# Rotary halves in the two late layers: matrix products on TensorE replaced by exchanges on SyncE's DMA queue, and four key products made two

## The reference, cut to what matters

```python
def apply_rope(x, cos, sin):
    x1, x2 = jnp.split(x, 2, axis=-1)
    rot = jnp.concatenate([-x2, x1], axis=-1)
    return x * cos + rot * sin

def apply_axial_rope(x, row_cs, col_cs):          # kind A, on each half of a head of 64
    half = x.shape[-1] // 2
    return concat([apply_rope(x[..., :half], *row_cs), apply_rope(x[..., half:], *col_cs)])

kv = einsum('bsr,rc->bsc', rms_norm(ckv, c_kvn), c_wukv).reshape(b, s, C_HEADS, C_NOPE + C_V)
kc_nope = kv[..., :C_NOPE]                        # the latent keys: 4 heads of 64 features
```

## Time and profile before

| what | value |
|---|---|
| median of three executions | 1819.11 us |
| the profiled execution's own time | 1817.71 us |
| its span in the profile | 1815.9 us |
| TensorE busy | 1764.0 us (97%) |
| VectorE, ScalarE, GpSimd busy | 797.8, 722.8, 603.9 us |
| mean granted TensorE clock | 0.989 of full speed |

### The profile page before, as it was taken

One profiled execution on the slowest core, in us unless ns is written; L12 is line 12 of the kernel. 1 busy time (PEld: TensorE's weight loads), 2 busy tenths in 40 slices (PEclk: granted clock), 3 DMA queues, 4 the chain that ended last, 5 costly groups with the idle time before them and its releaser, 6 DMA issues.

```text
span 1815.9 us, 25198 instructions
## 1 busy us (share of the span) xinstructions
PE 1764.0 (97%) x10862; PEld 1389.8 (77%) x10862; DVE 797.8 (44%) x1342; ACT 722.8 (40%) x1228; POOL 603.9 (33%) x182
## 2 busy tenths in 40 slices
PE   8999999999999999998999999989999999999997
PEld 5778899987888888877888888878675478766456
DVE  7756656623123120113680044135636654526653
ACT  5746565433233332223331122224336543345541
POOL 3434210333333334433354444433432115233112
PEclk9999999999999999998999999989999999999999
DMA  5130200315223322222232222223220012211001
GB/s 206 70 94 24 73 3 25 133 70 192 80 96 105 122 70 99 110 71 92 79 106 93 93 93 95 105 79 118 93 70 24 1 47 99 93 50 67 1 1 47
DMA packets 37503, 144.70 MB, mean 80 GB/s; under 512 B 3155, under 2 KB 15835, under 8 KB 23696
## 3 DMA queue, kind: packets, MB, share of 16 engines
q1 hardware_dynamic: 18944, 121.53, 18.7%
q10 hardware_dynamic: 18448, 21.57, 4.0%
HBM read 140.93 MB, written 5.30 MB: 81 GB/s over the span
## 4 chain that ended last, share of the span: by engine, by line
PE 91%; DVE 4%; ACT 2%; issue 1%; DMA 1%; ACTq 0%; POOL 0%; POOLq 0%; SPq 0%; DVEq 0%
PE bank L407 57%; PE bank L1145 7%; PE bank L613 5%; PE bank L418 4%; PE bank L2196 3%; PE bank L2220 3%; PE bank L2203 2%; PE bank L1653 1%; PE bank L1629 1%; PE bank L668 1%; PE bank L2228 1%; PE bank L2149 1%; ACT w_part L365 1%; PE bank L439 1%; DVE WK L978 0%
## 5 line engine op out<-in xcount | busy, mean ns | idle before, releaser
L407 PE MATMUL bank<-x_part,w_part 128*128 128x512 f32 x3216 | 747.1, 392 | 1.6 <-ACT WK L2309 0.8
L407 PEld LDWEIGHTS bank<-x_part,w_part 128*128 128x128 f32 x3216 | 601.2, 188 | 135.3 <-issue 10.3
L2660 POOL TENSOR_TENSOR w_part<-RAW,w_part 128x2048 fp32r<-128x2048 f32 (+1 forms) x90 | 404.2, 4494 | 676.6 <-ACT w_part L365 674.7
L365 ACT ACTIVATE w_part<-RAW 128x2048 fp32r<-128x2048 f32 (+1 forms) x90 | 165.8, 1842 | 176.3 <-PE bank L407 138.0
L2660 POOL TENSOR_TENSOR w_part<-WK,w_part 128x2048 fp32r<-128x2048 f32 (+1 forms) x30 | 123.7, 4123 | 248.6 <-ACT w_part L365 248.6
L407 PE MATMUL bank<-f_part,w_part 128*128 128x512 f32 x768 | 174.4, 389 | 0.0
L407 PEld LDWEIGHTS bank<-f_part,w_part 128*128 128x128 f32 x768 | 144.1, 188 | 29.9
L1145 PE MATMUL bank<-WK 64*64 64x64 f32 (+1 forms) x1456 | 102.0, 248 | 5.1 <-ACT WK L1311 3.4
L1145 PEld LDWEIGHTS bank<-WK 64*64 64x64 f32 (+1 forms) x1456 | 97.8, 162 | 7.3 <-ACT WK L1311 3.5
L978 DVE SCALAR_TENSOR_TENSOR WK<-bank,COL,WK 128x510 f32<-128x510 f32 (+1 forms) x96 | 71.7, 748 | 48.1 <-ACT WK L920 45.5
L2677 POOL TENSOR_TENSOR WK<-BASE,WK 128x1024 f32<-128x1024 f32 x16 | 30.4, 1898 | 160.0 <-DVE WK L2503 111.8
(11 more groups left out here) (286 smaller groups left out, 2230.8 us busy)
## 6 DMA issues: line engine op xcount, KB each, us to landing
RAW<-wts SPq DMA_DIRECT2D x83, 1024.0 KB, 4.8
WK<-wts SPq DMA_DIRECT2D x23, 1024.0 KB, 4.8
WK<-scratch ACTq DMA_DIRECT2D x16, 256.0 KB, 2.7
WK<-decay_rows ACTq DMA_DIRECT2D x14, 256.0 KB, 6.9
RAW<-wts SPq DMA_DIRECT2D x7, 512.0 KB, 3.5
WK<-wts SPq DMA_DIRECT2D x7, 512.0 KB, 3.4
scratch<-bias_rows ACTq DMA_DIRECT2D x4, 768.0 KB, 9.8
WK<-xT SPq DMA_DIRECT2D x4, 512.0 KB, 6.0
```

The lines of the kernel that those rows point to most:

```text
L365: act.eng.activation(high_part(i), raw_part(i), ACT.Copy).then_inc(*act.did(("hi", i)))
L407: mm = pe.eng.matmul(b[:, :], W[w][:, k, c:c + P], src[x][k], start=start and k == 0 and n == 0, stop=stop and k == kn - 1 and n == 2)
L2660: eng.tensor_tensor(low_part(i), raw_part(i), high_part(i).bitcast(F32), ALU.subtract).then_inc(w_split, 1)
```

## The change

1. Within each head of 64 the features of the kinds A and B are reordered on the host, so that the partner of a feature always lies 32 partitions away (`HALVES`, for A; B has that distance already). The cosine and sine tables are reordered alike, and the sign of the half turn moves into the sine tables.
2. The eight rotation products of a layer, and the matrices `ra` and `rb`, are gone. In their place SyncE issues eight DMAs per layer, SBUF to SBUF, four for `QKF` tiles 0 to 3 and four for tiles 4 to 7. Each moves 32 partitions by 4 x 512 float32 (256 KB) to the neighbouring 32 partitions of `XCH`, which is the place of the gates' tile `GTM`, still unused then. They stand in the queue just ahead of the load of the second piece of G0.
3. VectorE's `rope` reads `XCH` in place of PSUM. Rotations 0 to 3 stand ahead of the first `grow`, 4 to 6 behind the first three, 7 behind the fifth.
4. ScalarE's squares of C no longer wait for `ropes`. TensorE waits for it ahead of the attention.
5. The four latent key products of 64 rows become two of 128 rows; ScalarE still makes four copies, two from each.

```diff
-            pe.wait_ge(*at(("tabs", l)))
             pe.wait_ge(*at(("small", l)))
-            for i in range(8):
-                pe.wait_ge(*at((L, "qn", i)))
-                b = job((L, "rot", i))
-                E.matmul(b[:, :], tab("ra") if i < 4 else tab("rb"), QKF[:, i, :], start=True, stop=True).then_inc(*pe.did(("pe", (L, "rot", i))))
             for i in range(3):
                 fm((L, "C", i), f"L{l}C", i * P, HTS)
...
-            for h in range(4):
-                b = job((L, "uk", h))
-                E.matmul(b[0:64, :], UKV[:, h * 64:(h + 1) * 64], CL[:, 2, :], start=True, stop=True).then_inc(*pe.did(("pe", (L, "uk", h))))
+            for j in range(2):
+                b = job((L, "uk", j))
+                E.matmul(b[:, :], UKV[:, j * P:(j + 1) * P], CL[:, 2, :], start=True, stop=True).then_inc(*pe.did(("pe", (L, "uk", j))))
             gates(0)
             gates(1)
 
             pe.wait_ge(*at((L, "kready")))
             pe.wait_ge(*at((L, "qready")))
+            pe.wait_ge(*at((L, "ropes")))
...
             for i, m in enumerate((P, 64, P)):
-                act.wait_ge(*at((L, "ropes")))
                 act.wait_ge(*at((L, "ccp", i)))
...
-            def rope(dst, rot, c, s, tmp, m, rel, lab):
-
-                dve.wait_ge(*at(("pe", rot)))
-                V.tensor_tensor(tmp[0:m], ps(rot)[0:m, :], s[0:m], ALU.mult).then_inc(*dve.did(free=rot))
-                V.tensor_tensor(dst[0:m], dst[0:m], c[0:m], ALU.mult).then_inc(*dve.did())
+            def rope(i):
+
+                k = i // 4
+                x, y = QKF[:, i, :], XCH[:, i, :]
+                dve.wait_ge(*at(("turned", l, k)))
+                V.tensor_tensor(y, y, tab(("asn", "bs")[k]), ALU.mult).then_inc(*dve.did())
+                V.tensor_tensor(x, x, tab(("ac", "bc")[k]), ALU.mult).then_inc(*dve.did())
                 dve.wait_ge(*dve.last())
-                V.tensor_tensor(dst[0:m], dst[0:m], tmp[0:m], ALU.add).then_inc(*dve.did(*lab))
+                V.tensor_tensor(x, x, y, ALU.add).then_inc(*dve.did(*([(L, "ropes")] if i == KO - 1 else [])))
...
-            for j in range(4):
+            for i in range(4):
+                rope(i)
+            for j in range(3):
                 grow(j)
+                rope(4 + j)
+            grow(3)
             for h in range(4):
                 dve.wait_ge(*at((L, "cqc", h)))
             rope_c(CQ, SQL, 4, [(L, "qready")])
-            for j in range(4, KO):
+            grow(4)
+            rope(7)
+            for j in range(5, KO):
                 grow(j)
...
+            exchange_at = {(f"L{l}G0", 256): l for l in range(LAYERS)}
             for i, (_, _, k, n) in enumerate(subs):
+                if subs[i][:2] in exchange_at:
+                    l = exchange_at[subs[i][:2]]
+                    sp.wait_ge(*at(("pe", (f"lay{l}", "sum", 0))))
+                    for h in range(2):
+                        for j in range(4 * h, 4 * h + 4):
+                            sp.wait_ge(*at((f"lay{l}", "qn", j)))
+                        for b in range(4):
+                            frm = b ^ 1
+                            eng.dma_start(XCH[32 * b:32 * b + 32, 4 * h:4 * h + 4, :], QKF[32 * frm:32 * frm + 32, 4 * h:4 * h + 4, :])\
+                                .then_inc(turned_in[l][h], 16)
                 if i >= RAW_SLOTS:
                     sp.wait_ge(*at(("subfree", i - RAW_SLOTS)))
```

More of the change, by code:

```diff
@@ L50 @@
 TURNED = [*range(16, 32), *range(16)]
+HALVES = [*range(16), *range(32, 48), *range(16, 32), *range(48, 64)]
 MIXED = [12, 13, 6, 9, 0, 3, 14, 15, 7, 10, 1, 4, 8, 11, 2, 5]
@@ L117, in rope_tables @@
     return np.cos(ang).T.astype(np.float32), np.sin(ang).T.astype(np.float32)
[L120 to L129, removed]
 def shape_constants():
@@ L150, in shape_constants @@
     for n in range(2):
-        ax = np.concatenate([axr[n], axc[n]], 0)
+        ax = np.concatenate([axr[n], axc[n]], 0)[HALVES]
         tabs.append(np.concatenate([ax, ax], 0))
@@ L154, in shape_constants @@
         tabs.append(np.concatenate([one_d[n], one_d[n]], 0))
+    for x in (tabs[1], tabs[3]):
+        x[0:32] *= -1.0
+        x[64:96] *= -1.0
     for n in range(2):
@@ L168 @@
 TAB = dict(ac=(0, 512), asn=(512, 512), bc=(1024, 512), bs=(1536, 512), cc=(2048, 512), cs=(2560, 512),
-           ra=(3072, 128), rb=(3200, 128), win=(3328, 384))
-NTAB = 3712
+           win=(3072, 384))
+NTAB = 3456
 NGDN = 7 * P + 64
@@ L320, in build @@
         bias_in = [sem(f"bias_in{i}") for i in range(2)]
+        turned_in = [[sem(f"{k}_halves_exchanged{l}") for k in "ab"] for l in range(LAYERS)]
         out_done = sem("out_done")
@@ L323, in build @@
         rows_in = [sem(f"decay_rows_in{u}") for u in range(8)]
-        for s in [rows_out, bias_rows_out, *rows_in, *w_in_slot, w_split, const_in, gdnc_in, wgate_in, sel_in, *x_in, x_again, tabs_in, *small_in, *bias_out, *bias_in, out_done]:
+        for s in [rows_out, bias_rows_out, *rows_in, *w_in_slot, w_split, const_in, gdnc_in, wgate_in, sel_in, *x_in, x_again, tabs_in, *small_in, *bias_out, *bias_in, *turned_in[0], *turned_in[1], out_done]:
             byname[s.name] = s
@@ L341, in build @@
             table[("small", l)] = (small_in[l], 16)
+            for k in range(2):
+                table[("turned", l, k)] = (turned_in[l][k], 64)
         def weights(chunk, c):
@@ L2069, in build @@
         GTM = wk(25600, KO, S)
+        XCH = GTM
         MIX = parts("mix_part", 15360, KO, S)
@@ L2307, in lay_act @@
             for h in range(4):
-                act.wait_ge(*at(("pe", (L, "uk", h))))
-                A.activation(CK[0:64, h, :], ps((L, "uk", h))[0:64, :], ACT.Copy).then_inc(*act.did(*([(L, "kready")] if h == 3 else []), free=(L, "uk", h)))
+                j, o = divmod(h, 2)
+                act.wait_ge(*at(("pe", (L, "uk", j))))
+                A.activation(CK[0:64, h, :], ps((L, "uk", j))[64 * o:64 * o + 64, :], ACT.Copy)\
+                    .then_inc(*act.did(*([(L, "kready")] if h == 3 else []), free=(L, "uk", j) if o else None))
             for g in range(2):
@@ L2417, in lay_dve @@
             dve.wait_ge(*at(("tabs", l)))
-            def rope(dst, rot, c, s, tmp, m, rel, lab):
-                dve.wait_ge(*at(("pe", rot)))
-                V.tensor_tensor(tmp[0:m], ps(rot)[0:m, :], s[0:m], ALU.mult).then_inc(*dve.did(free=rot))
-                V.tensor_tensor(dst[0:m], dst[0:m], c[0:m], ALU.mult).then_inc(*dve.did())
+            def rope(i):
[4 more added lines that the diff above has]
+                V.tensor_tensor(x, x, tab(("ac", "bc")[k]), ALU.mult).then_inc(*dve.did())
                 dve.wait_ge(*dve.last())
-                V.tensor_tensor(dst[0:m], dst[0:m], tmp[0:m], ALU.add).then_inc(*dve.did(*lab))
+                V.tensor_tensor(x, x, y, ALU.add).then_inc(*dve.did(*([(L, "ropes")] if i == KO - 1 else [])))
             for i in range(4):
                 dve.wait_ge(*at(("pe", (L, "ass", i))))
-            for i in range(8):
-                rope(QKF[:, i, :], (L, "rot", i), tab("ac" if i < 4 else "bc"), tab("asn" if i < 4 else "bs"), SQL[:, i % 4, :], P, None,
-                     [(L, "ropes")] if i == 7 else [])
             for i in range(3):
@@ L2731, in part @@
         w = w2[l][:, SPLIT2[n]:SPLIT2[n] + width]
+        if n in ("aq", "ak"):
+            w = w.reshape(D, width // 64, 64)[:, :, HALVES].reshape(D, width)
         return w if order is None else np.concatenate([w[:, h * 64:h * 64 + 64] for h in order], 1)
```

5 lines of the change are left out of this document (2 added, 3 removed).

## The result

The changed kernel takes 1797.66 us in the median of four executions (1797.11 to 1802.15), the kernel before 1817.69 us (1815.01 to 1819.88, with a fourth execution beside the three shown above). The ratio is 0.9902 with a 95% interval of 0.989 to 0.9915: between 15 and 20 us less. The profiled execution took 1797.33 us, its span is 1795.5 us.

The account below looks back on a forecast made before the run. TensorE, busy 97% of the span, was taken as the bound; 13.6 us (rotations) plus 4.4 (key products) gave 18.0 off 1817.7, so 1799.7, or 1801.1 us as median. Own range 1797.5 to 1803.5, wider range to 1809.

Parts of the forecast that it names:

- The rotations leave TensorE: Between B3 and C0, removing the rotation products saves 6.5 to 7.1 us a layer, taken as 6.8, in all 13.6 us.
- The key products: Ahead of G0, two products replacing four save 2.6 us in layer 0 and 1.8 in layer 1, 4.4 us together.
- The sum: TensorE's list gets 18.0 us shorter: 13.6 from the rotations plus 4.4 from the key products.
- The exchanges cost nothing: SBUF-to-SBUF DMAs in SyncE's queue take 5.2 us pipelined, up to twice that, and cost TensorE nothing.
- before 1287: Sign that the forecast is right: the exchanges land before 1287 us on the timeline.
- over 12 us in all, the forecast fails: Sign that the forecast is wrong: the exchanges of a layer take over 12 us in all.
- The slack that I gave the G0 piece: The second G0 load, behind the exchanges, takes 4.8 us alone against 9.9 allowed: 5.1 us of slack.
- The deadline, 9.9 us after the load's issue: The second G0 piece must land by about 1292.2, 9.9 us after issue, for ScalarE to round it before C's sums.
- VectorE: 7.0 us early with the last rotation: At the gates, VectorE finishes rotation 7 at 1358.4, 7.0 us before TensorE asks for `ropes`, despite GpSimd locks.
- The rivals: Exchanges slightly late, 8 in 100; VectorE late at gates, 9; weights' queue chokes, 5; change not doing what it says, 2.
- the slower one: SyncE's queue chokes behind the exchanges: TensorE stands 42 us a layer, 1885 us, deciding beyond 9 us per layer; 5 in 100.
- The total: Whole kernel: 1799.7 us for the profiled execution, 1801.1 us in terms of the median; 76 in 100.

Follow-up runs that it names:

- no_exchange: The changed kernel without the sixteen exchange DMAs and VectorE's wait for them, so rotations take stale data for their second term: 1800.48 us, ratio 0.9916.
- held_c0: The changed kernel with SyncE holding the exchanges until TensorE has finished C0: 1797.92 us, ratio 0.9894 to the kernel before.
- held_c1: The changed kernel with SyncE holding the exchanges until TensorE has finished C1: 1826.13 us, ratio 1.0046 to the kernel before.
- rotations_late4: The changed kernel with rotations 4 to 7 together behind the large latent rotation, ahead of the fifth gate scaling: 1797.51 us, ratio 0.9889.
- neighbours: The changed kernel with partner features on neighbouring partitions, two DMAs of 64 partitions in steps of two replacing four of 32: 1799.33 us, ratio 0.9912.
- rotations_ahead_of_c: The changed kernel with all eight VectorE rotations ahead of the scaling of C, exchanges awaited there: 1823.74 us, ratio 1.0042 to the kernel before.

## Why the prediction was right, point by point

- **The rotations leave TensorE: 6.8 us a layer.** Measured 6.87 in both, and nothing of it comes back behind. The share of 0.3 us for the float32 products' edges was real: 6.47 us were their own.
- **The key products: 2.6 and 1.8 us.** Measured 2.65 and 1.85 up to the first logits, so the term was right. The sign given for it was not: I expected about 1.8 us from their start to G0's, and it is 1.42, below my lower bound of 1.6. G0 starts early and the gate products take 0.3 to 0.4 us longer, which the prediction didn't foresee.
- **The sum: 18.0 us.** Measured 18.2 from B3 of layer 0 to the first logits of layer 1.
- **The exchanges cost nothing.** Right, by `no_exchange` and by the stretches. But their length was wrong: I took the pipelined 5.2 us, "up to twice its value". In the changed kernel the last exchange is issued at 1275.3 and lands 8.7 us later, at 1284.0. On the clock of the kernel before that is 1287.1, 10.9 us after the point from which I counted, and just past the "before 1287" that I gave as a sign. From the first issue (1268.70) it is 15.3 us, with the G0 load ahead of them still under way; read so, my "over 12 us in all, the forecast fails" was a false alarm. The slack that I gave the G0 piece, 5.1 us, was 1.3 in fact. The rule of the Trainium skill that I put beside the sum ("SBUF — State Buffer", section "Door 1: The DMA port swizzle") gave an end at 1286 to 1287 and "about 1 us of slack", and was close. That the term stayed at nothing is therefore partly luck: it rested on a slack four times the real one.
- **The deadline, 9.9 us after the load's issue.** With the piece 1.3 us early there the changed kernel shows 8.6 + 1.3 = 9.9; `held_c0` reaches it in layer 0.
- **VectorE: 7.0 us early with the last rotation.** Measured 7.0. I had counted the locks of the first rotation and of `rope_c` and left room for one at the gates; the trace has just these three.
- **The rivals.** None came. The price of the slower one was wrong in kind: I reckoned a microsecond of TensorE's time for each of stall. `held_c1` shows 13.7 us for a stall of 4.5, as the clock falls. The point from which it decides lies therefore not at 9 us of stall a layer but below 4: both layers' stalls of 4.5 and 3.5 us already made the kernel 0.46% slower than before. I had given it 5 in 100 and 42 us of stall; a tighter transfer than I thought stood before a steeper edge than I thought.
- **The total.** For the profiled execution 1799.7 us was forecast and 1797.33 came, 2.4 us less. Of these 0.2 us are the terms of the sum, 3.1 us are B3's earlier start and 1.0 us, the other way, is the end of the program. The last two are scatter, and they happened to leave the time inside the forecast's own range. In terms of the median 1801.1 us was forecast, from the 1819.11 us of three executions. With the fourth that median is 1817.69, which makes the same forecast 1799.7, against 1797.66 measured.

No run beat the changed kernel clearly. `rotations_late4` and `held_c0` lie within 0.3 us of it. `neighbours` has the same time with more room in the queue, and would be the one to build on.

## What to carry to other kernels

Work that only moves data between partitions can leave a bound TensorE for the DMA queue, if what reads it is moved to where it is needed last: the same exchange awaited some 30 us earlier turned a gain of 1% into a loss of 0.4%. The price to work out is not the transfer but what stands behind it in the same queue, with its deadline. And spread an SBUF-to-SBUF copy over all partitions, in steps if need be: the same bytes then moved at 410 GB/s in place of 235.

## What the runs showed of the hardware that I had not expected

- A stall of TensorE can cost more than itself. After waits of 3.5, 4.5 and 8.9 us the matmuls that followed ran at a granted clock of 0.50 (`held_c1`: for 19 us; `rotations_ahead_of_c`: 0.53 over the 7 us behind the wait, 1.00 after it), after a wait of 0.59 us they did not. After one and the same wait of 1.5 us near the end of the program the clock was 1.00 in the kernel before and 0.68 in the changed one. The Trainium skill, "TensorE: Matmul & The Clock Gate", states that idle stretches bring the clock to its lower level; these waits agree, and the rivals' prices should have held it. What I had not expected at all is how long it stayed down: in `held_c1` the query and key products ran without a gap for 19 us and the clock was back only behind the start of the gate products (0.82 from 1323.6 to 1326.0, then 1.00).
- SyncE's issue of an exchange takes 0.58 to 1.82 us in layer 0 of the changed kernel, 0.77 in the median, where a load of four times the bytes takes 0.33. Eight of them hold the queue for 7.6 us, four of twice the partitions for 2.7 (`neighbours`).
- From SBUF to SBUF, copies of 32 adjacent partitions moved 235 GB/s and copies of 64 in steps of two 410 GB/s, with the DMA engines fully busy in both.
